# A store of 128 equal rows in place of a flip by matmuls: relative-position bias tables in a decoder trunk

## The chip, the cores and the metric

The kernel runs on one core of a Trainium2 chip. The metric is the device time of one execution in microseconds (us). The program is written out engine by engine: TensorE (PE in the profile, PEld for its weight loads), VectorE (DVE), ScalarE (ACT), GpSimd (POOL), and SyncE (SP), whose queue issues every DMA of this kernel. The engines meet only through semaphores.

## The reference

One pre-norm layer over 512 tokens of width 2048, in float32: three groups of heads on one input projection (6 gated DeltaNet heads, 4 dilated-window softmax heads, 6 sparse-attention heads), an output projection, and a gated MLP. The part that matters here is the bias of the ten softmax heads. It depends only on the distance between query and key:

```
def rel_bucket(dist):
    max_exact = REL_BUCKETS // 2
    n = jnp.maximum(dist, 0)
    nf = jnp.maximum(n, 1).astype(jnp.float32)
    large = max_exact + (jnp.log(nf / max_exact) / math.log(REL_MAX_DIST / max_exact)
                         * (REL_BUCKETS - max_exact)).astype(jnp.int32)
    large = jnp.minimum(large, REL_BUCKETS - 1)
    return jnp.where(n < max_exact, n, large)
...
            logits = (jnp.einsum('bhqd,bhqjd->bhqj', qb, kg)
                      + tab[:, rel_bucket(dil * j)][None, :, None, :])
...
        logits = jnp.einsum('bgrqd,bgkd->bgrqk', qb, kb) + w_bias
```

So head h needs, for query row p of a block of 128 and column c, a value f_h(p - c + constant): a table in which each row is the row above it, moved by one column.

## The kernel before

The work is a chain of blocks. At the end of a block all engines wait for each other, and the next block starts only then. The first block (the L322 block) normalizes x, transposes it on TensorE and splits it into a high and a low part (`h_hi`, `h_lo`), and makes the bias tables. The second (the L412 block) is the DeltaNet heads, the third (L935) the four dilated heads, the fourth (L1042) the sparse heads; output projection and MLP follow. Through all of them one stream of weights flows: SyncE loads units of 1 MB into two buffers `w_raw` (`load_unit`, L146), ScalarE rounds quarters of them to `w_hi` (L173), VectorE takes the rest into `w_lo` (L182), and TensorE multiplies them with three matmuls for each 128 rows of the contraction (`project`, L221). The independent projections are laid between the dependent steps of the heads (`filler`), so that TensorE nearly always has something to do.

The bias tables take this way in the first block:

1. TensorE makes for each of the ten heads one row of 1024 values (two matmuls, L391), and VectorE copies them to SBUF into `rev`, which is rows 0 to 9 of the tile `onehot` (L379, L380).
2. SyncE stores these 10 rows of 4 KB to the DRAM scratch `rev_d` (L351; `bias_scratch` in the profile), and waits until they have landed.
3. SyncE reads them back in 16 pieces of up to 512 columns. Row p of a piece begins one element after row p-1: the step between rows is 1 (L356). The pieces lie where `xs`, the input, was, and so each round of 8 waits until x was used. Between the two rounds it loads the first two weight units.
4. The rows come out in the wrong order (the first should be the last). So TensorE multiplies each piece with a matrix `K_REV` that flips the 128 rows (L406), and VectorE copies the result back (L385). These are the last thing that both do in the block.
5. SyncE stores the 16 pieces to a second scratch, `toep_d` (L362; `toeplitz_scratch`), and waits at the end of the block until all have landed.

Block three loads the tables of its four heads with one DMA (L989, `dil_tab`), block four those of its six heads with one (L1210, `nsa_tab`), as aligned rows. Everything SyncE issues stands in one queue, in the order of the program. What is in that queue in the first block is the order of the `@block.sync` function below. ScalarE and VectorE have split eight quarters, two weight units, by the end of the first block; TensorE uses up one of the two there (L398) and starts the second block with the other.

Of the kernel before, what the change touches and what calls it, by code (L numbers as in the profile page):

```python
# [22 lines left out]
F32 = mybir.dt.float32  # L23
# [5 lines left out]
P = 128  # L29
# [5 lines left out]
DN_H, DIL_H, NSA_H, NSA_G = 6, 4, 6, 2  # L35
# [15 lines left out]
QW = 512  # L51
RING = 8
AHEAD = 4
TW_DIL, TW_NSA = 512, 896
YLEN = 1024
# [2 lines left out]

LEVELS = (2, 4, 8, 16, 32, 64)

(K_ID, K_ONE, K_TRI, K_ML, K_MU, K_M1, K_M1T, K_REV) = range(8)
K_LV = 8
N_CST = K_LV + len(LEVELS)

N_SMALL = 2 * DN_H + 3 * NSA_H
# [40 lines left out]
def program(nc, t):  # L106
    with ExitStack() as ctx:
        def sem(name):
            return ctx.enter_context(nc.semaphore(name))
# [10 lines left out]
        cst = sb(ctx, "cst", [P, N_CST, P])  # L120
# [3 lines left out]
        PB, W = bank[:4], bank[4:]  # L124
        ident, ones = cst[:, K_ID, :], cst[:, K_ONE, :]
        ob = [sb(ctx, f"head_out{g}", [P, SEQ]) for g in range(NSA_G)]
        mix_d = nc.dram_tensor("mix_scratch", (KT, P, SEQ), F32).ap()
        rev_d = nc.dram_tensor("bias_scratch", (DIL_H + NSA_H, YLEN), F32)


        raw_in = [sem("raw_in_even"), sem("raw_in_odd")]
# [110 lines left out]
        const_in, table_in = sem("const_in"), sem("table_in")  # L242
        stored = sem("stored")
# [70 lines left out]

        toep_d = nc.dram_tensor("toeplitz_scratch", (DIL_H + NSA_H, P, TW_NSA), F32).ap()

        PIECES = [(h, 0, QW) for h in range(DIL_H + NSA_H)] + [(h, QW, TW_NSA - QW) for h in range(DIL_H, DIL_H + NSA_H)]
        ROUNDS = (PIECES[:8], PIECES[8:])  # L320

        with ExitStack() as c1, nc.Block() as block:  # L322
            xs = sb(c1, "xs1", [P, TB, D_MODEL])
            bl, oh = sb(c1, "bias_lhs", [BUCKETS + 2, DIL_H + NSA_H]), sb(c1, "onehot", [BUCKETS + 2, YLEN])
            rev = oh[0:DIL_H + NSA_H, :]
            id1 = sb(c1, "ident_first", [P, P])

            def piece(i, w):

                return xs[:, i // 4, i % 4 * QW:i % 4 * QW + w]  # L330

            x_in = [sem(f"x_in{b}") for b in range(TB)]
            const_ready, id_in, bias_in, rev_ps, rev_sb, piece_ps, piece_sb = (
                sem(n) for n in ("const_ready", "id_in", "bias_in", "rev_ps", "rev_sb", "piece_ps", "piece_sb"))
            g_row, g_in = sb(c1, "n1_g", [P, D_MODEL]), sem("n1_g_in")
            n1_act, n1_dve, n1_pe, n1_y, n1_lo = normalize(
                "n1", lambda e, b: e.wait_ge(x_in[b], 16), g_row, g_in, xs, c1, id1[:])

            @block.sync
            def _(sp):  # L340
                sp.dma_start(bl[:], t["bias_lhs"]).then_inc(bias_in, 16)
                sp.dma_start(oh[:], t["onehot"]).then_inc(bias_in, 16)
                sp.dma_start(xs[:, 0, :], t["x"][0:P, :]).then_inc(x_in[0], 16)
                sp.dma_start(id1[:], t["cst"][:, K_ID, :]).then_inc(id_in, 16)
                sp.dma_start(g_row[:], t["g1"]).then_inc(g_in, 16)
                sp.dma_start(xs[:, 1, :], t["x"][P:2 * P, :]).then_inc(x_in[1], 16)
                sp.dma_start(cst[:], t["cst"]).then_inc(const_in, 16)
                for b in range(2, TB):
                    sp.dma_start(xs[:, b, :], t["x"][b * P:(b + 1) * P, :]).then_inc(x_in[b], 16)
                sp.wait_ge(rev_sb, 1)  # L350
                sp.dma_start(rev_d.ap()[:, :], rev).then_inc(stored, 16)  # L351
                sp.wait_ge(stored, 16)
                for r, pieces in enumerate(ROUNDS):
                    sp.wait_ge(n1_y, 8 * (r + 1))
                    for i, (h, c, w) in enumerate(pieces):
                        sp.dma_start(piece(8 * r + i, w), bass.AP(tensor=rev_d, offset=h * YLEN + c, ap=[[1, P], [1, w]]))\  # L356
                            .then_inc(table_in, 16)
                    if r == 0:
                        load_units(sp, 2)
                for i, (h, c, w) in enumerate(PIECES):  # L360
                    sp.wait_ge(piece_sb, i + 1)
                    sp.dma_start(toep_d[h, :, c:c + w], piece(i, w)).then_inc(stored, 16)  # L362
                sp.wait_ge(stored, 16 + 16 * len(PIECES))

            @block.gpsimd
            def _(pool):
                nc.gpsimd.memset(eps_t[:], EPS).then_inc(const_ready, 1)
                nc.gpsimd.memset(one_t[:], 1.0).then_inc(const_ready, 1)

            @block.scalar  # L370
            def _(act):
                act.wait_ge(const_ready, 2)
                n1_act(act)
                split_hi(act, AHEAD + 4)

            @block.vector
            def _(dve):
                dve.wait_ge(rev_ps, 1)
                step(nc.vector.tensor_copy(rev[:, 0:512], W[0][0:DIL_H + NSA_H, :]))  # L379
                nc.vector.tensor_copy(rev[:, 512:1024], W[1][0:DIL_H + NSA_H, :]).then_inc(rev_sb, 1)  # L380
                n1_dve(dve)
                split_lo(dve, AHEAD + 4)
                for i, (h, c, w) in enumerate(PIECES):
                    dve.wait_ge(piece_ps, i + 1)
                    nc.vector.tensor_copy(piece(i, w), W[i % 4][:, 0:w]).then_inc(piece_sb, 1)  # L385

            @block.tensor
            def _(pe):
                pe.wait_ge(bias_in, 32)
                for i in range(2):  # L390
                    m = nc.tensor.matmul(W[i][0:DIL_H + NSA_H, :], bl[:], oh[:, i * 512:(i + 1) * 512],  # L391
                                         start=True, stop=True)
                m.then_inc(rev_ps, 1)
                pe.wait_ge(id_in, 16)
                n1_pe(pe)

                pe.wait_ge(n1_lo, 4 * TB)
                filler(pe, 1)(KT)  # L398
                pe.wait_ge(const_in, 16)
                pe.wait_ge(rev_sb, 1)  # L400
                for i, (h, c, w) in enumerate(PIECES):
                    if i % 8 == 0:
                        pe.wait_ge(table_in, 16 * (i + 8))
                    if i >= 4:
                        pe.wait_ge(piece_sb, i - 3)
                    nc.tensor.matmul(W[i % 4][:, 0:w], cst[:, K_REV, :], piece(i, w), start=True, stop=True)\  # L406
                        .then_inc(piece_ps, 1)

        STORED2 = 16 + 16 * len(PIECES)


        with ExitStack() as c2, nc.Block() as block:  # L412
# [522 lines left out]
        with ExitStack() as c3, nc.Block() as block:  # L935
            tab = sb(c3, "dil_tab", [P, DIL_H, TW_DIL])
# [31 lines left out]
            def dil_dve(dve, n, hd):  # L968
                settle(dve)
                dve.wait_ge(q_used, Q3 + 12 * n)  # L970
                nc.vector.tensor_scalar(qs[:], PB[0][:], SCALE, None, ALU.mult).then_inc(q_ev, 1)
                split_lo(dve, 2)
                dve.wait_ge(table_in, 16 * len(PIECES) + 16)

                def bias(a, e):
                    if isinstance(hd, int):
                        return tab[:, hd, a:e]
                    return tab[:, bass.ds(hd, 1), a:e].rearrange("p a n -> p (a n)")

                attend_dve(dve, n, lg, nm, den, bias, None, True, lambda k: split_lo(dve, 2 * k))  # L980
                split_lo(dve, 2)
                dve.wait_ge(att_o, n + 1)
                dve.wait_ge(stored, 16 * DN_H + STORED2 + 16 * n)
                nc.vector.tensor_copy(ob[0][:], PB[3][:]).then_inc(ob_v, 1)
                dve.wait_ge(ob_v, n + 1)

            @block.sync
            def _(sp):
                sp.dma_start(tab[:], toep_d[0:DIL_H, :, 0:TW_DIL].rearrange("h p c -> p h c")).then_inc(table_in, 16)  # L989
                for n in range(DIL_H):  # L990
                    load_units(sp, (Q3 + 12 * (n + 1) + AHEAD + 3) // 4)
                    sp.wait_ge(ob_v, n + 1)
                    sp.dma_start(mix_d[DN_H + n, :, :], ob[0][:]).then_inc(stored, 16)
# [48 lines left out]
        with ExitStack() as c4, nc.Block() as block:  # L1042
# [162 lines left out]
            def _(sp):  # L1205
# [1 line left out]
                sp.dma_start(w2[:], t["cmp_w2"]).then_inc(par4, 16)  # L1207
                load_units(sp, (Q_HEAD + AHEAD + 3) // 4)
                sp.wait_ge(q_used, Q_CMP + 2 * W1Q)
                sp.dma_start(tab[:], toep_d[DIL_H:, :, :].rearrange("h p c -> p h c")).then_inc(table_in, 16)  # L1210
                for r in range(NSA_R):
                    load_units(sp, (Q_HEAD + 8 * min(r + 1, NSA_R - 1) + AHEAD + 3) // 4)
                    if r == NSA_R - 1:
# [97 lines left out]
            def _(dve):  # L1311
# [50 lines left out]
                for g in range(NSA_G):  # L1362
                    dve.wait_ge(cm_k, 2 + g)
                    nc.vector.tensor_copy(vc[:, g, :], W[2 + g][0:N_CMP, 0:HD]).then_inc(cm_kv, 1)
                dve.wait_ge(table_in, 16 * len(PIECES) + 32)
                take_q(dve, 0)
                with repeat(dve, NSA_R - 1, (dve_q, 8, "nsa_dve quarters"), (dve_c, TICKS["nsa_dve"], "nsa_dve")) as r:
                    nsa_dve(dve, r, False)
# [294 lines left out]
def constant_tiles():  # L1663
# [9 lines left out]
    out[:, K_ML] = np.where(i > j, 0, BIG)  # L1673
    out[:, K_MU] = np.where(i <= j, 0, -BIG)
    out[:, K_M1] = level(1)
    out[:, K_REV] = i + j == P - 1
    out[:, K_M1T] = level(1).T
    for n, b in enumerate(LEVELS):
        out[:, K_LV + n] = level(b).T
# [107 lines left out]
```

## Time and profile before

| | us |
|---|---|
| median of 3 runs | 2793.23 (2792.86 to 2794.67) |
| the profiled execution, its own time | 2789.81 |
| its span in the trace | 2788.0 |
| granted TensorE clock, mean | 0.975 |
| TensorE busy | 2628.1 (94% of the span) |
| VectorE busy | 1315.3 (47%) |
| ScalarE busy | 874.3 (31%) |
| DMA: all queues | 259.34 MB, 93 GB/s on average |

The span begins with the first instruction that the trace shows. What lies between the span and the time of the execution is 1.8 us. The share of a DMA row is the mean over the core's 16 DMA engines.

### The profile page before, as it was taken

How to read it: one execution, taken by the hardware profiler on the slowest of the kernel's cores; microseconds unless marked ns; L12 is line 12 of the kernel's file. 1: busy time of each engine (PE TensorE's matmuls, PEld its weight loads, DVE VectorE, ACT ScalarE, POOL GpSimd, SP SyncE). 2: the span in 40 equal slices, each digit the busy share in tenths (PEclk: the TensorE clock that was granted, in tenths of full speed). 3: DMA queues.
4: the chain of work that ended last, by engine and by line, in shares of the span. 5: the costliest groups of instructions: out<-in, count | busy, mean ns of one | idle time of the engine just before them, and what ended most of it. 6: DMA issues, size and time to landing. Idle time of an engine off the chain costs nothing.

```text
span 2788.0 us, 33817 instructions
## 1 busy us (share of the span) xinstructions
PE 2628.1 (94%) x12024; PEld 2124.7 (76%) x12024; DVE 1315.3 (47%) x2196; ACT 874.3 (31%) x1628; POOL 77.0 (3%) x54
## 2 busy tenths in 40 slices
PE   6999989889999886998999999999999999999997
PEld 4777777777788553886888888888888888888886
DVE  5555666633244555334444444444344444444444
ACT  3433333323234333223332223232223232323223
POOL 0001111100000000000000000000000000000002
PEclk9999999999999996998999999999999999999999
DMA  6111111112235001521322222222222223222222
GB/s 239 72 65 34 60 64 64 49 65 98 76 117 208 14 38 68 204 99 57 110 101 98 97 91 91 106 94 103 91 91 91 102 95 106 91 92 103 91 94 91
DMA packets 44219, 259.34 MB, mean 93 GB/s; under 512 B 5136, under 2 KB 7056, under 8 KB 15292
## 3 DMA queue, kind: packets, MB, share of 16 engines
q1 hardware_dynamic: 44092, 257.62, 25.7%
q8 instruction: 83, 1.36, 0.2%
q14 instruction: 44, 0.36, 0.0%
HBM read 245.37 MB, written 12.23 MB: 92 GB/s over the span
## 4 chain that ended last, share of the span: by engine, by line
PE 52%; DVE 0%; ACT 0%; issue 0%; DVEq 0%; ACTq 0%
PE bank L221 34%; PE bank L1502 18%; ACT fin_squares L1606 0%; DVE xs L1649 0%; DVE xs L1648 0%; DVE xs L1564 0%; DVEq L1467 0%; ACT fin_rs L1609 0%; ACT L1609 0%; DVE fin_rs L1643 0%; ACTq L1605 0%; DVEq L1628 0%
## 5 line engine op out<-in xcount | busy, mean ns | idle before, releaser
L221 PE MATMUL bank<-h_hi,w_hi 128*128 128x512 f32 x2272 | 915.4, 403 | 12.2 <-DVE w_lo L182 6.9
L221 PE MATMUL bank<-h_lo,w_hi 128*128 128x512 f32 x2272 | 889.3, 391 | 0.0
L221 PE MATMUL bank<-h_hi,w_lo 128*128 128x512 f32 x2272 | 888.5, 391 | 0.0
L182 DVE TENSOR_TENSOR w_lo<-w_raw,w_hi 128x512 fp32r<-128x512 f32 x840 | 557.4, 711 | 470.5 <-ACT w_hi L173 468.9
L173 ACT ACTIVATE w_hi<-w_raw 128x512 fp32r<-128x512 f32 x840 | 489.5, 624 | 707.5 <-PE bank L1502 314.9
L221 PEld LDWEIGHTS bank<-h_hi,w_hi 128*128 128x128 f32 x2272 | 429.4, 189 | 103.0 <-issue 10.2
L221 PEld LDWEIGHTS bank<-h_lo,w_hi 128*128 128x128 f32 x2272 | 428.7, 189 | 91.8
L221 PEld LDWEIGHTS bank<-h_hi,w_lo 128*128 128x128 f32 x2272 | 429.5, 189 | 86.7 <-issue 3.2
L1502 PE MATMUL bank<-w_lo,g_hi 128*128 128x512 f32 x704 | 279.1, 396 | 0.0
L1502 PE MATMUL bank<-w_hi,g_lo 128*128 128x512 f32 x704 | 279.1, 396 | 0.0
L1502 PE MATMUL bank<-w_hi,g_hi 128*128 128x512 f32 x704 | 279.1, 396 | 0.0
L1564 DVE TENSOR_TENSOR xs<-xs,bank 128x512 f32<-128x512 f32 x176 | 120.9, 687 | 229.4 <-PE bank L1502 222.5
L1542 DVE SCALAR_TENSOR_TENSOR ffn_val<-bank,ffn_wg,ffn_val 128x511 f32<-128x511 f32 x44 | 33.0, 750 | 388.7 <-ACT ffn_val L1518 388.7
L1518 ACT ACTIVATE ffn_val<-bank,ffn_wg 128x512 f32<-128x512 f32 x44 | 30.3, 689 | 425.2 <-PE bank L221 425.2
L1502 PEld LDWEIGHTS bank<-w_lo,g_hi 128*128 128x128 f32 x704 | 132.6, 188 | 32.3
L1502 PEld LDWEIGHTS bank<-w_hi,g_lo 128*128 128x128 f32 x704 | 132.6, 188 | 32.3
L1502 PEld LDWEIGHTS bank<-w_hi,g_hi 128*128 128x128 f32 x704 | 132.6, 188 | 32.3
L1407 PE MATMUL bank<-w_hi,h_hi 128*128 128x512 f32 x256 | 101.0, 394 | 2.0 <-DVEq L1430 2.0
L1407 PE MATMUL bank<-w_hi,h_lo 128*128 128x512 f32 x256 | 100.6, 393 | 0.0
L1407 PE MATMUL bank<-w_lo,h_hi 128*128 128x512 f32 x256 | 100.5, 393 | 0.0
L1624 POOL TENSOR_TENSOR xs<-xs,gain_row 128x512 f32<-128x512 f32 x12 | 16.4, 1400 | 2200.9 <-ACT fin_squares L1606 2200.9
L790 POOL TENSOR_TENSOR dn_LT<-dn_AT,cst 128x512 f32<-128x512 f32 x36 | 60.3, 1709 | 488.2 <-ACT dn_AT L678 488.2
(274 smaller groups left out, 1992.3 us busy)
## 6 DMA issues: line engine op xcount, KB each, us to landing
w_raw<-in_weights SPq DMA_DIRECT2D x210, 1024.0 KB, 4.8
xs<-in_x SPq DMA_DIRECT2D x4, 1024.0 KB, 13.6
mix_scratch<-head_out SPq DMA_DIRECT2D x16, 256.0 KB
xs<-in_x SPq DMA_DIRECT2D x1, 4096.0 KB, 17.7
out<-xs SPq DMA_DIRECT2D x4, 1024.0 KB, 6.1
nsa_tab<-toeplitz_scratch SPq DMA_DIRECT2D x1, 2688.0 KB, 11.2
xs<-bias_scratch SPq DMA_DIRECT2D x10, 256.0 KB, 5.1
toeplitz_scratch<-xs SPq DMA_DIRECT2D x10, 256.0 KB
```

The costliest lines, as they stand in the source:

```text
L173: nc.scalar.activation(w_hi[:, act_q.n % RING, :], raw_quarter(act_q), ACT.Copy)\
L182: nc.vector.tensor_tensor(w_lo[:, s, :], raw_quarter(dve_q), w_hi[:, s, :].bitcast(F32), ALU.subtract).then_inc(lo_done, 1)
L221: m = nc.tensor.matmul(PB[pb][:], a[:, s, k], b[:, kt, :], start=(kt == 0 and n == 0), stop=(kt == KT - 1 and n == 2))
L790: nc.gpsimd.tensor_tensor(v3(LT[:, lv, :]), v3(B["AT"][:]), c3b(K_LV + lv), ALU.mult)\
L1407: m = nc.tensor.matmul(bank[4 * c + b][:], x[:, kt, b * P:(b + 1) * P], w[:, s, :], start=(kt == 0 and n == 0), stop=(kt == KT - 1 and n = ...
L1502: m = nc.tensor.matmul(W[b][:], x[:, slot, kt, b * P:(b + 1) * P], w[:, s, :], start=(kt == 0 and n == 0), stop=(kt == GT - 1 and n == 2))
L1518: nc.scalar.activation(dst[:], PB[2 * (j % 2) + v][:], ACT.Copy, scale=fwg[:, v, 2, j:j + 1])\
L1542: link(dve, nc.vector.scalar_tensor_tensor(dst[:, 1:SEQ], bk[:, 0:SEQ - 1], fwg[:, v, 1, j:j + 1], dst[:, 1:SEQ], ALU.mult, ALU.add))
L1564: nc.vector.tensor_tensor(dst, dst, W[b][:], ALU.add).then_inc(dn_free, 1)
L1624: nc.gpsimd.tensor_tensor(xs[:, b, cc], xs[:, b, cc], fg[:, cc], ALU.mult).then_inc(fin_g, 1)
```

## The change

The ten rows of 1024 are stored 128 times each: `rows_d` (`bias_rows` in a profile) holds 128 equal rows of 4 KB for each head, 5.24 MB in all, written by one DMA whose source repeats each SBUF row (step 0, count 128). From such a scratch a table in the right order can be read straight: it begins in the first row at column 127, and the step from row to row is 1023, one whole row less one element. So the pieces, the flip, its copies, the second scratch and the matrix `K_REV` are gone. Block three reads its tables with four DMAs instead of one, block four with six instead of one. The two weight units of the first block are now loaded ahead of the wait for `rev`. SyncE still waits in the first block until the store has landed.

```
-        rev_d = nc.dram_tensor("bias_scratch", (DIL_H + NSA_H, YLEN), F32)
+        rows_d = nc.dram_tensor("bias_rows", (DIL_H + NSA_H, P, YLEN), F32)
...
-        PIECES = [(h, 0, QW) for h in range(DIL_H + NSA_H)] + [(h, QW, TW_NSA - QW) for h in range(DIL_H, DIL_H + NSA_H)]
-        ROUNDS = (PIECES[:8], PIECES[8:])
+        STORED2 = 16
+
+        def load_table(sp, tab, heads, width):
+
+            for i, h in enumerate(heads):
+                src = bass.AP(tensor=rows_d, offset=h * P * YLEN + P - 1, ap=[[YLEN - 1, P], [1, width]])
+                sp.dma_start(tab[:, i, :], src).then_inc(table_in, 16)
...
+                load_units(sp, 2)
                 sp.wait_ge(rev_sb, 1)
-                sp.dma_start(rev_d.ap()[:, :], rev).then_inc(stored, 16)
-                sp.wait_ge(stored, 16)
-                for r, pieces in enumerate(ROUNDS):
-                    sp.wait_ge(n1_y, 8 * (r + 1))
-                    for i, (h, c, w) in enumerate(pieces):
-                        sp.dma_start(piece(8 * r + i, w), bass.AP(tensor=rev_d, offset=h * YLEN + c, ap=[[1, P], [1, w]]))\
-                            .then_inc(table_in, 16)
-                    if r == 0:
-                        load_units(sp, 2)
-                for i, (h, c, w) in enumerate(PIECES):
-                    sp.wait_ge(piece_sb, i + 1)
-                    sp.dma_start(toep_d[h, :, c:c + w], piece(i, w)).then_inc(stored, 16)
-                sp.wait_ge(stored, 16 + 16 * len(PIECES))
+                sp.dma_start(rows_d.ap()[:, :, :], rev[:, None, :].to_broadcast([DIL_H + NSA_H, P, YLEN]))\
+                    .then_inc(stored, 16)
+                sp.wait_ge(stored, STORED2)
...
-                for i, (h, c, w) in enumerate(PIECES):
-                    dve.wait_ge(piece_ps, i + 1)
-                    nc.vector.tensor_copy(piece(i, w), W[i % 4][:, 0:w]).then_inc(piece_sb, 1)
...
-                for i, (h, c, w) in enumerate(PIECES):
-                    if i % 8 == 0:
-                        pe.wait_ge(table_in, 16 * (i + 8))
-                    if i >= 4:
-                        pe.wait_ge(piece_sb, i - 3)
-                    nc.tensor.matmul(W[i % 4][:, 0:w], cst[:, K_REV, :], piece(i, w), start=True, stop=True)\
-                        .then_inc(piece_ps, 1)
...
-                sp.dma_start(tab[:], toep_d[0:DIL_H, :, 0:TW_DIL].rearrange("h p c -> p h c")).then_inc(table_in, 16)
+                load_table(sp, tab, range(DIL_H), TW_DIL)
...
-                sp.dma_start(tab[:], toep_d[DIL_H:, :, :].rearrange("h p c -> p h c")).then_inc(table_in, 16)
+                load_table(sp, tab, range(DIL_H, DIL_H + NSA_H), TW_NSA)
```

SyncE's queue in the first block of the kernel before, from the load of the constants (`cst`) to the first load of block two. `x2` is two alike in a row; a wait stands with the row that it holds.

```order
L347 DMA cst<-in_cst 128x1792
L349 DMA xs<-in_x 128x2048 x2
L351 DMA bias_scratch<-onehot 10x1024 [waits rev_sb]
L356 DMA xs<-bias_scratch 128x512 [waits n1_y,stored]
L356 DMA xs<-bias_scratch 128x512 x7
L146 DMA w_raw<-in_weights 128x2048 x2
L356 DMA xs<-bias_scratch 128x512 [waits n1_y]
L356 DMA xs<-bias_scratch 128x512
L356 DMA xs<-bias_scratch 128x384 x6
L362 DMA toeplitz_scratch<-xs 128x512 [waits piece_sb] x10
L362 DMA toeplitz_scratch<-xs 128x384 [waits piece_sb] x6
L322 UNCONDITIONAL_BRANCH [waits stored]
```

The same stretch of the changed kernel:

```order
L346 DMA cst<-in_cst 128x1664
L348 DMA xs<-in_x 128x2048 x2
L146 DMA w_raw<-in_weights 128x2048 x2
L351 DMA bias_rows<-onehot 1280x1x1024 [waits rev_sb]
L325 UNCONDITIONAL_BRANCH [waits stored]
L771 UNCONDITIONAL_BRANCH [waits barrier_Pool_Activation_PE_DVE_SP_release]
L773 DMA small_raw<-in_w_small 128x480
```

The two weight loads now stand right behind those of x; one store of 1280 rows of 1024 is all that remains of 33 DMAs, and the branch behind it still waits for `stored` and ends the block.

TensorE's queue at the end of the first block, as a difference: the last projection, the flip, and the branches to the next block.

```order
 L221 MATMUL bank<-h_hi,w_lo 128x512
 L221 MATMUL bank<-h_lo,w_hi 128x512
-L406 MATMUL bank<-xs,cst 128x512 x10
-L406 MATMUL bank<-xs,cst 128x384 x6
-L322 UNCONDITIONAL_BRANCH
-L809 UNCONDITIONAL_BRANCH
```

The 16 flips are gone, so the last work of TensorE in the first block is the last matmul of the projection.

## Rows read from the trace of the kernel before

**Rows 1.** The page: busy time, share, instructions; the chain by engine.

```profile
PE 2628.1 (94%) x12024; PEld 2124.7 (76%) x12024; DVE 1315.3 (47%) x2196; ACT 874.3 (31%) x1628; POOL 77.0 (3%) x54
...
PE 52%; DVE 0%; ACT 0%; issue 0%; DVEq 0%; ACTq 0%
```

**Rows 2.** Timeline of the first block: start, duration, engine, instruction, idle before.

```profile
11.51 0.67 DVE L380 COPY onehot<-bank 10x512 f32<-10x512 f32 x1
12.21 0.30 SPq L351 DMA_DIRECT2D bias_scratch<-onehot  x1
...
22.03 3.67 SPq L356 DMA_DIRECT2D xs<-bias_scratch  x8
25.74 1.01 SPq L146 DMA_DIRECT2D w_raw<-in_weights  x2
...
35.67 4.26 ACT L173 ACTIVATE w_hi<-w_raw 128x512 fp32r<-128x512 f32 x8
...
49.63 0.39 PE L221 MATMUL bank<-h_lo,w_hi 128*128 128x512 f32 x1
...
49.86 12.62 PE L406 MATMUL bank<-xs,cst 128*128 128x512 f32 x32
...
65.37 0.34 SPq L795 DMA_DIRECT2D small_raw<-in_w_small  x1
65.41 0.65 PE L221 MATMUL bank<-h_hi,w_hi 128*128 128x512 f32 x1 [2.94 <-PEq L322]
```

**Rows 3.** The DMA queue's own waits over the span: us, times, longest.

```profile
SPq L356 <- DMA bias_scratch<-onehot: 1.5, 1, 1.5
SPq L322 <- DMA toeplitz_scratch<-xs: 1.5, 1, 1.5
```

**Rows 4.** DMA packets in the stretch 18.5 to 19.25 us.

```profile
DMA packets 47, 0.16 MB, mean 208 GB/s; under 512 B 24, under 2 KB 24, under 8 KB 32
```

**Rows 5.** DMA packets in the stretch 21.2 to 21.5 us.

```profile
DMA packets 5, 0.01 MB, mean 27 GB/s; under 512 B 3, under 2 KB 3, under 8 KB 5
```

**Rows 6.** Stretches: busy us by engine, granted clock, DMA share, GB/s.

```profile
19.00:21.20 2.20, 0.41 (x3) 0.04 (x2) 2.20 (x5) 1.94 (x3) 0.00 (x0) 1.00 0.13 52
24.00:28.00 4.00, 2.34 (x16) 1.68 (x15) 4.00 (x8) 3.75 (x6) 0.00 (x0) 1.00 1.03 300
65.40:69.00 3.60, 3.59 (x9) 2.83 (x10) 0.37 (x1) 0.60 (x1) 0.00 (x0) 0.53 0.59 110
69.00:75.00 6.00, 6.00 (x28) 4.97 (x27) 0.29 (x1) 0.00 (x0) 0.00 (x0) 1.00 0.79 332
890.00:892.00 2.00, 2.00 (x11) 1.63 (x10) 0.93 (x3) 0.03 (x1) 0.00 (x0) 1.00 0.98 414
```

**Rows 7.** DMA issues: how many, KB each, median us to landing.

```profile
nsa_tab<-toeplitz_scratch SPq DMA_DIRECT2D x1, 2688.0 KB, 11.2
...
dil_tab<-toeplitz_scratch SPq DMA_DIRECT2D x1, 1024.0 KB, 5.5
...
onehot<-in_onehot SPq DMA_DIRECT2D x1, 136.0 KB
```

**Rows 8.** Timeline where the third block begins, to TensorE's first turn.

```profile
596.83 0.38 SPq L989 DMA_DIRECT2D dil_tab<-toeplitz_scratch  x1
...
604.92 1.15 ACT L173 ACTIVATE w_hi<-w_raw 128x512 fp32r<-128x512 f32 x2 [5.52 <-DMA w_raw<-in_weights]
...
606.79 0.28 DVE L890 TENSOR_TENSOR dil_lg<-bank,dil_tab 128x128 f32<-128x128 f32 x1
...
610.67 0.29 DVE L899 TENSOR_SCALAR dil_lg<-dil_lg,dil_den 128x128 f32<-128x128 f32 x1
...
611.15 0.27 PE L869 MATMUL bank<-cst,dil_lg 128*128 128x128 f32 x1
```

**Rows 9.** Tile nsa_tab: its load, and its first reader on VectorE.

```profile
L1172 DVE TENSOR_TENSOR cmp_lg<-bank,nsa_tab x24: 192/202/204, 915.8 to 1047.5; 128x31 f32<-128x31 f32 x24
...
L1210 SPq DMA_DIRECT2D nsa_tab<-toeplitz_scratch x1: 426/426/426, 891.1 to 891.1; - x1
```

More of the change, by code:

```diff
@@ L59 @@
 LEVELS = (2, 4, 8, 16, 32, 64)
-(K_ID, K_ONE, K_TRI, K_ML, K_MU, K_M1, K_M1T, K_REV) = range(8)
-K_LV = 8
+(K_ID, K_ONE, K_TRI, K_ML, K_MU, K_M1, K_M1T) = range(7)
+K_LV = 7
 N_CST = K_LV + len(LEVELS)
@@ L312, in normalize @@
             return act_part, dve_part, pe_part, y_v, lo
-        toep_d = nc.dram_tensor("toeplitz_scratch", (DIL_H + NSA_H, P, TW_NSA), F32).ap()
-        PIECES = [(h, 0, QW) for h in range(DIL_H + NSA_H)] + [(h, QW, TW_NSA - QW) for h in range(DIL_H, DIL_H + NSA_H)]
-        ROUNDS = (PIECES[:8], PIECES[8:])
+        STORED2 = 16
[3 more added lines that the diff above has]
+                sp.dma_start(tab[:, i, :], src).then_inc(table_in, 16)
         with ExitStack() as c1, nc.Block() as block:
@@ L326, in program @@
             id1 = sb(c1, "ident_first", [P, P])
-            def piece(i, w):
-                return xs[:, i // 4, i % 4 * QW:i % 4 * QW + w]
             x_in = [sem(f"x_in{b}") for b in range(TB)]
-            const_ready, id_in, bias_in, rev_ps, rev_sb, piece_ps, piece_sb = (
-                sem(n) for n in ("const_ready", "id_in", "bias_in", "rev_ps", "rev_sb", "piece_ps", "piece_sb"))
+            const_ready, id_in, bias_in, rev_ps, rev_sb = (
+                sem(n) for n in ("const_ready", "id_in", "bias_in", "rev_ps", "rev_sb"))
             g_row, g_in = sb(c1, "n1_g", [P, D_MODEL]), sem("n1_g_in")
@@ L400, in _ @@
                 pe.wait_ge(rev_sb, 1)
-                for i, (h, c, w) in enumerate(PIECES):
-                    if i % 8 == 0:
-                        pe.wait_ge(table_in, 16 * (i + 8))
-                    if i >= 4:
-                        pe.wait_ge(piece_sb, i - 3)
-                    nc.tensor.matmul(W[i % 4][:, 0:w], cst[:, K_REV, :], piece(i, w), start=True, stop=True)\
-                        .then_inc(piece_ps, 1)
-        STORED2 = 16 + 16 * len(PIECES)
         with ExitStack() as c2, nc.Block() as block:
@@ L972, in dil_dve @@
                 split_lo(dve, 2)
-                dve.wait_ge(table_in, 16 * len(PIECES) + 16)
+                dve.wait_ge(table_in, 16 * DIL_H)
                 def bias(a, e):
@@ L1364, in _ @@
                     nc.vector.tensor_copy(vc[:, g, :], W[2 + g][0:N_CMP, 0:HD]).then_inc(cm_kv, 1)
-                dve.wait_ge(table_in, 16 * len(PIECES) + 32)
+                dve.wait_ge(table_in, 16 * (DIL_H + NSA_H))
                 take_q(dve, 0)
@@ L1675, in constant_tiles @@
     out[:, K_M1] = level(1)
-    out[:, K_REV] = i + j == P - 1
     out[:, K_M1T] = level(1).T
```

## The prediction

> **What bounds the kernel now.** I read the page first. TensorE is busy 94% of the span and the chain of work that ended last lies on it alone [rows 1]. So a change counts only where TensorE stands still or does work that can go. The timeline of the first block shows both. The last projection ends at 49.63 + 0.39 = 50.0 us, then the flips run for 12.6 us, and the next projection starts at 65.41 after 2.94 us without work [rows 2]. Those 2.94 us come from SyncE: it issues the last store, waits 1.5 us for it [rows 3], then the blocks change. What stands between the last projection of block one and the first of block two is 65.4 - 50.0 = 15.4 us, and all of it belongs to the tables.
>
> **What is removed.** The flips, their copies, the pieces and the second store go. If nothing else held the block, it would end with the projection. What stays is the change of blocks itself. Of the 2.94 us, 1.5 are the landing, about 0.7 the last copy (as L380) and 0.3 the last issue (as L351) [rows 2, 3]; 0.5 us is left for it. TensorE would then restart at 50.5 instead of 65.4: 14.9 us less. It would also start warm. In the kernel before, the pause is followed by 3.6 us at a granted clock of 0.53, that is at the lower of its two levels, 1.2 GHz, for nearly all of it: 9 matmuls in 3.6 us, 0.40 each, where the next 28 take 6.0 us, 0.21 each, at 2.4 GHz [rows 6]. That is another 9 x 0.19 = 1.7 us. The gain without any wait for the store is 16.6 us.
>
> **What is added: one store.** SyncE still waits for it before it leaves the block, so its landing is the other thing that can end the block. Three things fix it.
>
> *When it starts.* It is issued at 12.2 us as before [rows 2], but all DMAs stand in one queue, and each DMA engine works its part in order. The kernel before shows this: the 40 KB of the old store were issued at 12.21, and SyncE saw them land at 22.03, 9.5 us later, the last 1.5 of them after nothing else was left to wait for [rows 2, 3]. Their ten packets of 4 KB leave when the loads of x have drained: eight in the stretch to 19.25 us (32 packets under 8 KB less 24 tiny ones) [rows 4] and two at 21.2 to 21.5 us (5 less 3) [rows 5]. In between, the DMA share is 0.13, two engines of 16, at 52 GB/s [rows 6]: two engines run late. Now two weight units, 2.1 MB, stand ahead of the store. One engine moves 414 / (0.98 x 16) = 26.4 GB/s [rows 6], and its part of 131 KB takes 5.0 us. The store starts at about 18.9 + 5.0 = 23.9 us on most engines, 26.3 on the two late ones.
>
> *On how many engines it runs.* The ten old packets went to the late pair and to eight others, one row to an engine: ten engines. The new store has the same ten source rows, so I count 128 packets of 4 KB, 524 KB, for each of ten engines. At 26.4 GB/s that is 19.9 us.
>
> *Whether ten neighbouring SBUF rows can feed ten engines.* No row shows this: the old store took one packet from each row and was over before a limit could show, and every transfer at full rate in this trace covers 128 SBUF rows. There, 16 engines and 128 rows are the same thing, eight rows to an engine, and 26.4 GB/s may be the limit of the engine or that of a path into SBUF which serves eight rows. If it is the engine's, the store takes 19.9 us. If it is the path's, what counts is how many of rows 0 to 9 share one: 2, 4 or 8 of them, for 39.8, 79.4 or 159 us. These are the bounds, 19.9 and 159. I take four, the middle one of the three splits that share. The Trainium skill, page "SBUF — State Buffer", section "Door 1: The DMA port swizzle", maps rows 0 to 3 to one port, 4 to 7 to another and 8 and 9 to a third, each of about 27 GB/s, and says that a narrow tile reaches only these ports; by it the sum is 79 us too, and by the count of engines alone it would be 20. No run shown here confirms that for a store.
>
> *Sum with four rows to a path.* 23.9 + 79.4 = 103.3 us; SyncE sees it 0.5 us later (21.5 to 22.03 above); 0.5 us for the barrier: block two starts at 104.3. TensorE stands still from 50.0 on, and restarts cold as it did before, so the clock gives nothing back. Against 65.4 this is +38.9 us. DVE, ACT and TensorE all have their next work behind the block's end, and nothing in block two can be brought forward, so no cover exists for it.
>
> **What moves: the weight loads.** They land before 24 us instead of after 30; ScalarE takes them at 35.67 in both cases, straight after its last piece of h [rows 2]. No gain. They don't delay x, which stands ahead of them.
>
> **What moves: the table reads.** Block three issues four DMAs in place of one, at about 0.46 us each (3.67 for eight [rows 2]), 1.4 us more for SyncE, but the DMA engines are still at the table then, so the weight unit behind it isn't held by the issue. The skewed reads of the old pieces ran at 300 GB/s, in the stretch 24 to 28 us [rows 6], where aligned loads make 414: 1 MB in 3.5 us, not 2.5. Behind the table waits the weight unit for ScalarE (604.92), then VectorE (606.79, and 610.67 + 0.29), then TensorE at 611.15 [rows 8], with 0.2 us to spare. So 0 to 0.8 us; if all of the issue came on top, 2. The old pieces of a head read one and the same 4 KB, the new ones distinct rows, so I take 0.4. In block four the table is issued at 891.1, lands 11.2 us later and is first read at 915.8 [rows 7, 9]: 13 us of room, against 5 x 0.46 = 2.3 of issue and about 2.5 of slower reading. Nothing.
>
> Sum: 38.9 + 0.4 = +39.3 us. The profiled execution would go from 2789.8 to 2829.1, and the median, which lies 3.4 above, from 2793.2 to about 2832.
>
> **The rivals.**
>
> *Ten engines at full rate.* The store lands at 23.9 + 19.9 = 43.8 us, on the late pair 46.2, plus 0.5: 46.7, before TensorE's 50.0. Then the gain is whole: -16.6 + 0.4 = -16.2, 2777 us. For it speaks that the old packets left on eight engines within the same 0.75 us [rows 4]; against it, that they may have been fetched earlier, while the loads ahead of them were still being written, so that one packet each proves little. This is the case on the other side. It decides as long as sharing costs less than (49.5 - 24.4) / 19.9 = 1.26 times the unshared time.
>
> *Two rows to a path.* 23.9 + 39.8 + 1.0 = 64.7 us, the same as 65.4 before: with the tables -0.3, 2793 us. The whole gain would be eaten, and TensorE would stand still where it flipped.
>
> *Eight rows to a path.* 23.9 + 159 + 1.0 = 184: +118.5 + 0.4, 2912 us.
>
> *The tables are late.* If the skewed reads were much slower than 300 GB/s, block three would pay. At half that rate 1 MB takes 7 us, 4.5 more: +4.3 us on top of any case. Distinct rows a whole row apart speak against it.
>
> **How the numbers follow.** Four rows 0.60; ten engines at full rate 0.27; two rows 0.08; eight rows or worse 0.05. A measurement of this kernel tells 0.2% (5.6 us) from no change. So slower 0.65, same 0.08, faster 0.27. The time is that of the likeliest, 2832. Its own range is 2824 to 2841 (the start of the store 3 us either way, the rate 25.5 to 27.2 GB/s, the tables 0 to 4). To hold 8 in 10 the range must take in the unshared case: 2774 to 2841.
>
> **What would show it.** In the profile after: a gap of TensorE behind its first projection, ended by the change of blocks, about 54 us long (no gap, or one under 1 us, for ten engines at full rate; 14 for two rows). SyncE waits for the DMA of `bias_rows` to about 104 us. The slices from 24 to 103 us show a low DMA rate: with ports shared some 66 GB/s (5.24 MB in 79 us), with ten engines 264 GB/s until 44 us and then nothing. Block two starts at 104 instead of 65.4, and everything behind it keeps its length, up to 1 us at 600. Wrong would be a store that spreads over another number of engines than ten, or one limited by neither engine nor path but by the DRAM side.

## The result, and the profile after

| | before | after |
|---|---|---|
| median | 2793.05 us (2792.00 to 2794.67, 4 runs) | 2838.85 us (2834.94 to 2839.31, 4 runs) |
| ratio, 95% interval | | 1.0160 (1.0143 to 1.0178) |
| profiled execution, its span | 2789.81, 2788.0 | 2834.94, 2833.2 |
| granted clock, mean | 0.975 | 0.967 |

The changed kernel is 1.6% slower: 45.8 us by the medians, 45.2 by the spans of the two traces.

The page of the changed kernel, busy time of the engines (against [rows 1]), and its largest group with the idle time in front of it and what ended that:

```profile
PE 2615.3 (92%) x11992; PEld 2114.8 (75%) x11992; DVE 1305.4 (46%) x2180; ACT 874.9 (31%) x1628; POOL 77.0 (3%) x54
...
L221 PE MATMUL bank<-h_hi,w_hi 128*128 128x512 f32 x2272 | 915.2, 403 | 65.3 <-PEq L325 55.8
```

TensorE works 13 us less than before and the kernel takes 45 us more: what came is a wait. Most of it is one wait of 55.8 us, ended by the change of blocks (line 325). The timeline shows where it lies (start, duration, engine, instruction, idle before it; against [rows 2]):

```profile
5.00 0.93 SPq L146 DMA_DIRECT2D w_raw<-in_weights  x2
11.89 0.94 SPq L351 DMA_DIRECT2D bias_rows<-onehot  x1
34.36 4.26 ACT L173 ACTIVATE w_hi<-w_raw 128x512 fp32r<-128x512 f32 x8
...
48.55 0.39 PE L221 MATMUL bank<-h_lo,w_hi 128*128 128x512 f32 x1
104.75 0.34 SPq L773 DMA_DIRECT2D small_raw<-in_w_small  x1
104.79 0.77 PE L221 MATMUL bank<-h_hi,w_hi 128*128 128x512 f32 x1 [55.85 <-PEq L325]
```

SyncE's own waits in the first 120 us say what it waited for at that line (us, times, longest; against [rows 3]):

```profile
SPq L325 <- DMA bias_rows<-onehot: 91.5, 1, 91.5
```

And three stretches: busy us by engine, then granted clock, DMA share and GB/s (the third against [rows 6]):

```profile
28.00:60.00 32.00, 16.73 (x72) 12.90 (x70) 12.26 (x20) 8.22 (x15) 0.00 (x0) 0.82 0.60 77
62.00:102.00 40.00, 0.00 (x0) 0.00 (x0) 0.00 (x0) 0.00 (x0) 0.00 (x0) 0.50 0.48 51
104.80:108.50 3.70, 3.70 (x9) 2.93 (x10) 0.00 (x0) 0.25 (x1) 0.00 (x0) 0.51 0.55 107
```

The last columns are the ones to read. A share of 0.60 is 9.6 engines of 16 busy, so ten engines do have the store, and yet they move 77 GB/s together, 7.7 each, where an engine alone moved 26.4 [rows 6]. After 62 us 7.7 engines are busy with 51 GB/s. Engines that count as busy at a low rate point to a limit that isn't theirs; experiments 1 to 3 test that. The third stretch is TensorE after the pause, at a granted clock of 0.51, the lower of its two levels.

The whole difference, block by block, from the two traces (each stretch from the first row of a block to that of the next):

| stretch | before | after | difference |
|---|---|---|---|
| to the start of block two | 65.37 | 104.75 | +39.4 |
| block two | 531.46 | 531.59 | +0.1 |
| block three | 163.65 | 164.69 | +1.0 |
| block four | 357.17 | 355.97 | -1.2 |
| block five | 199.49 | 199.67 | +0.2 |
| MLP, to its first output store | 1459.05 | 1464.72 | +5.7 |

These make 45.2. Block four took between 356 and 360 us in all kernels of this study, those with the old tables too, so the -1.2 means nothing. Block two took between 530 and 535 us in them, so the +0.1 is closer than it deserves. The 5.7 us in the MLP are a surprise: the change touches nothing there.

### The profile page after: what moved, and what is told of

Its sections match the earlier page's. It is cut to its first block, busy times and chain, and to the rows that moved or that the text cites. A ratio compares the mean times of both kernels' runs of the same rounds, so it can differ in the third digit from the quotient of the medians.

```text
span 2833.2 us, 33712 instructions
## 1 busy us (share of the span) xinstructions
PE 2615.3 (92%) x11992; PEld 2114.8 (75%) x11992; DVE 1305.4 (46%) x2180; ACT 874.9 (31%) x1628; POOL 77.0 (3%) x54
## 3 DMA queue, kind: packets, MB, share of 16 engines
q8 instruction: 87, 1.43, 0.2%
## 4 chain that ended last, share of the span: by engine, by line
PE 51%; issue 0%; DVE 0%; ACT 0%; DVEq 0%; ACTq 0%
PE bank L221 34%; PE bank L1480 17%; ACT fin_squares L1584 0%; DVE xs L1627 0%; DVE xs L1626 0%; DVE xs L1542 0%; DVEq L1445 0%; ACT fin_rs L1587 0%; ACT L1587 0%; DVE fin_rs L1621 0%; ACTq L1583 0%; DVEq L1606 0%
## 5 line engine op out<-in xcount | busy, mean ns | idle before, releaser
L221 PE MATMUL bank<-h_hi,w_hi 128*128 128x512 f32 x2272 | 915.2, 403 | 65.3 <-PEq L325 55.8
```

Source lines behind the costliest of these rows:

```text
L221: m = nc.tensor.matmul(PB[pb][:], a[:, s, k], b[:, kt, :], start=(kt == 0 and n == 0), stop=(kt == KT - 1 and n == 2))
```

## The experiments

The theory was that a path into SBUF serves four neighbouring rows and that the store, with its ten sources in rows 0 to 9, has three such paths. The rivals: the limit is the count of engines, or lies on the DRAM side (128 equal rows written from one source). For the 5.7 us the theory was the place of the code, and the rival that the long pause or the changed buffers cause it. Where a time is from one execution it is given as "one run".

### 1. Source rows 12 apart

The matmul that makes the ten rows gets a wider left side with zero columns between the heads, and so puts them into rows 0, 12, ... 108 of a tile of their own. The DMA is otherwise the same: ten rows, 128 times.

```
+STEP = 12
+ROWS = 9 * STEP + 1
...
-            rev = oh[0:DIL_H + NSA_H, :]
+            rev = sb(c1, "bias_out", [ROWS, YLEN])
...
-                sp.dma_start(rows_d.ap()[:, :, :], rev[:, None, :].to_broadcast([DIL_H + NSA_H, P, YLEN]))\
+                sp.dma_start(rows_d.ap()[:, :, :], rev[0:ROWS:STEP, None, :].to_broadcast([DIL_H + NSA_H, P, YLEN]))\
```

> The changed kernel with its ten source rows at SBUF partitions 0, 12, 24, ... 108 instead of 0 to 9. The bytes, the ten engines and the packets of the store stay the same. Theory (neighbouring SBUF rows share a path of 26 GB/s): ten rows far apart share nothing, the store moves 264 GB/s and lands at about 46 us, block two starts at about 49.5 instead of 104.8 us, and the time is 2839 - 55 = 2784 us. Rival (ten engines, the repeated source or the DRAM side limit the store): nothing changes, 2839 us, block two at 104.8.

Measured: 2782.97 us (2779.1 to 2784.2, 6 runs) against 2793.49 of the kernel before (12 runs), ratio 0.9961 (0.9948 to 0.9974). The stretch of the store, columns as above:

```profile
26.00:42.00 16.00, 11.50 (x44) 9.53 (x45) 14.71 (x25) 9.99 (x19) 0.00 (x0) 0.61 0.64 264
```

Its timeline at the change of blocks:

```profile
50.49 0.39 PE L223 MATMUL bank<-h_lo,w_hi 128*128 128x512 f32 x1
51.17 0.34 SPq L775 DMA_DIRECT2D small_raw<-in_w_small  x1
...
51.20 0.47 PE L223 MATMUL bank<-h_hi,w_hi 128*128 128x512 f32 x1 [0.32 <-PEq L327]
```

The same ten engines (0.64 x 16 = 10.2) move 264 GB/s instead of 77, the ten times 26.4 of the prediction's first rival. The store is over at 46.1 us, before the projection, and TensorE waits 0.3 us instead of 55.8. One DMA with the same bytes, the same count of packets and the same target takes some 23 us from its first packet to its last, in place of 80, when its source rows have moved. (They also lie in a tile of their own now; experiments 2 and 3 have the same kind of tile and are slow.) The count of engines is not the limit, nor is the DRAM side, nor that each row is read 128 times. The MLP kept its extra time here (1464.99 us), so that does not come from the pause.

### 2. Source rows 2 apart

Experiment 1 with `STEP = 2`: rows 0, 2, ... 18. Groups of four rows make five pairs of them.

> The same with the ten source rows at partitions 0, 2, 4, ... 18. Theory (four neighbouring rows share a path): two rows share each path, the store takes 39.8 us instead of 79.4 and ends at about 63 us, block two starts at about 64 us, and the time is 2839 - 40 = 2799 us; the rate is 132 GB/s from start to end, since all five paths have the same load. If rows shared in groups of eight, 79 us and 2839 us; if the store were limited by anything but the rows, 2839 us as well.

Measured: 2801.33 us, one run. Stretch of the store, and TensorE's wait for the change of blocks:

```profile
28.00:60.00 32.00, 18.18 (x73) 14.74 (x71) 13.02 (x22) 8.35 (x15) 0.00 (x0) 0.71 0.60 126
```

```profile
PE bank L223 <- PEq L327: 16.0, 1, 16.0
```

126 GB/s on ten engines is five times 25.2, five paths. Groups of eight rows would have made only three. The prediction's rival "two rows to a path" had 64.7 us for the start of block two; it was 66.4, since one of the pairs lies on the two engines that start late: from 64 to 65 us only two engines were still busy (share 0.12), with 25 GB/s together.

### 3. Source rows 8 apart

`STEP = 8`: rows 0, 8, ... 72. No two of them are neighbours, so groups of four alone would give ten paths and 264 GB/s. This run asks whether rows far apart can share too. The Trainium skill says so ("SBUF — State Buffer", section "Door 1: The DMA port swizzle"): a row and the one 32 above it have the same port, one 64 above has another.

> As the spread by 12, but with the ten source rows at partitions 0, 8, 16, ... 72. No two of them are within four of each other. Theory A (only neighbours within a group of four or eight rows share a path): nothing shares, the store takes 20 us as with step 12, 2783 us. Theory B (the port map of the Trainium skill, page SBUF - State Buffer, Door 1: a row and the one 32 further on share a port, a row and the one 64 further on don't): rows 0 and 32, 8 and 40, 16 and 48, 24 and 56 share, rows 64 and 72 have a port each; eight of the ten engines run at half rate, the store takes 40 us, 145 to 160 GB/s at first, and the time is 2801 us, as with step 2.

Measured: 2796.81 us, one run (the kernel before 2787.79, one run). Two stretches of its store:

```profile
26.00:42.00 16.00, 12.10 (x50) 9.78 (x51) 14.30 (x25) 9.11 (x17) 0.00 (x0) 0.68 0.62 161
56.00:60.00 4.00, 0.00 (x0) 0.00 (x0) 0.00 (x0) 0.00 (x0) 0.00 (x0) 0.50 0.49 102
```

161 is six times 26.8, and later 102 is four times 25.5. The map of the Trainium skill gives just that: rows 0 and 32, 8 and 40, 16 and 48, 24 and 56 share, 64 and 72 stand alone. That makes six paths, of which the two with one row are done first. So "rows that are not neighbours" is no rule for spreading; a step of 12 works because it meets ten different paths.

### 4. One store of 40 KB, then a copy from DRAM to DRAM

The ten rows are stored once, and a second DMA writes each of them 128 times from there. It has 128 as its outer count instead of ten, and no SBUF side.

```
-        STORED2 = 16
+        STORED2 = 32
...
-                sp.dma_start(rows_d.ap()[:, :, :], rev[:, None, :].to_broadcast([DIL_H + NSA_H, P, YLEN]))\
-                    .then_inc(stored, 16)
+                sp.dma_start(one_d.ap()[:, :], rev).then_inc(stored, 16)
+                sp.wait_ge(stored, 16)
+                sp.dma_start(bass.AP(tensor=rows_d, offset=0, ap=[[YLEN, P], [P * YLEN, DIL_H + NSA_H], [1, YLEN]]),
+                             bass.AP(tensor=one_d, offset=0, ap=[[0, P], [YLEN, DIL_H + NSA_H], [1, YLEN]])).then_inc(stored, 16)
```

> The changed kernel, but SyncE stores the ten rows once (40 KB), waits, and repeats them 128 times by one DMA from DRAM to DRAM with the 128 copies as its outer dimension. Theory (the limit is on the SBUF side of the store): the copy runs on all 16 engines at the full rate, 5.24 MB in 12.7 us, over at about 41 us, before TensorE ends at 48.9; 2784 us, like the spread rows. Rival (writing 5.24 MB to DRAM in rows of 4 KB is what is slow, about 77 GB/s): 68 us for the copy, block two at about 97 us, 2831 us.

Measured: 2784.70 us (2782.2 to 2786.2, 7 runs) against 2793.49 (12 runs), ratio 0.9971 (0.9959 to 0.9982). Stretch of the copy, and SyncE's waits for the two DMAs:

```profile
30.00:42.00 12.00, 8.20 (x29) 6.90 (x30) 10.92 (x18) 6.77 (x13) 0.00 (x0) 0.54 1.02 322
```

```profile
SPq L326 <- DMA bias_rows<-bias_one: 19.2, 1, 19.2
SPq L354 <- DMA bias_one<-onehot: 14.4, 1, 14.4
```

All 16 engines are busy and write the same 5.24 MB at 322 GB/s, in about 17 us where 12.7 were expected. The 14.4 us are the small store's wait behind the loads of x and the weights. After it the copy still ends before the projection. So the DRAM takes such a stream at more than four times the 77 GB/s of the changed kernel.

### 5. The kernel before, with the new store added

Nothing is taken away: the old tables stay, and the new store, which nobody reads, is issued ahead of the pieces' stores; the block waits for both.

> The kernel before the change, with the new store of 5.24 MB added behind the loads of the second round of pieces, waited for at the end of block one and read by nobody. The part that the change adds, alone. Theory (four rows share a path): its packets start at about 40 us, it runs 79.4 us to 120 us, the stores of the flipped pieces queue behind it for 9 us more on the busy engines, and block two starts at about 129 us instead of 65.4: 2857 us, with no gaps in the MLP, since no code is moved. Rival (the store would be fast where it doesn't meet other traffic, ten engines at full rate): over at 60 us, hidden, 2793 to 2797 us.

Measured: 2860.72 us, one run, against 2791.14 (15 runs). Stretch of its store, and TensorE's wait:

```profile
44.00:60.00 16.00, 16.00 (x54) 9.91 (x53) 6.22 (x9) 0.00 (x0) 0.00 (x0) 1.00 0.60 77
```

```profile
PE bank L222 <- PEq L324: 67.9, 1, 67.9
```

Again 77 GB/s on ten engines, at another time, with TensorE at full clock beside it. The low rate belongs to the store, not to what ran beside it in the changed kernel. Block two began at 131.7 us, 66 later than before: the stores of the pieces stand behind the long one on the same engines and had to wait for it too.

### 6. The changed kernel, with 16 matmuls in the pause

Now the 5.7 us. In the changed kernel the MLP stretch has four gaps of TensorE that the kernel before has not, at 1710.7, 1976.0, 2241.6 and 2507.1 us, all in one line. The last one in the timeline, and the wait as the profile names it ("issue": nothing that the profile shows):

```profile
2507.12 0.39 PE L221 MATMUL bank<-h_hi,w_hi 128*128 128x512 f32 x1
2508.73 0.50 PE L221 MATMUL bank<-h_hi,w_lo 128*128 128x512 f32 x1 [1.22 <-issue]
```

```profile
PE bank L221 <- issue: 4.1, 4, 1.2
```

Two such matmuls follow at 0.23 us; here it is 1.61. The four together are 4.8 us over the normal step. The same stretch before and after:

```profile
1317.10:2776.20 1459.10, 1454.19 (x6336) 1191.68 (x6336) 645.72 (x1035) 423.75 (x737) 16.37 (x12) 1.00 0.27 96
```

```profile
1356.70:2821.40 1464.70, 1455.66 (x6336) 1190.90 (x6335) 646.04 (x1035) 423.72 (x737) 16.37 (x12) 1.00 0.27 95
```

The stretch is 5.6 us longer at the same granted clock, and the other engines worked as long as before. TensorE stood idle for 4.1 us more and counts 1.5 us more as busy; where the 0.8 us lie that the four gaps don't hold wasn't located.

The gaps lie 265.3, 265.6 and 265.5 us apart, once per pass of TensorE's loop in the MLP, and TensorE's program has become shorter ahead of that loop (32 matmuls and their 32 weight loads fewer). So the loop stands at another place of the code. The experiment puts 16 matmuls, with a result that nobody reads, into the pause of the first block, where they cost nothing:

```
                 pe.wait_ge(rev_sb, 1)
+                for i in range(16):
+                    nc.tensor.matmul(W[i % 4][:], cst[:, K_ONE, :], xs[:, i // 4, i % 4 * QW:(i % 4 + 1) * QW],
+                                     start=True, stop=True)
```

> The changed kernel with 16 more matmuls of TensorE behind its first projection, whose results nobody reads; TensorE stands still there anyway. It puts back the length of TensorE's program. It is for the 5 to 6 us that the changed kernel loses in the MLP, where its trace has four gaps of 1.2 to 1.6 us, one in each new pass of the loop, with no releaser. Theory (where the program's code falls decides whether a pass waits for code): the gaps are gone and the time is 2839 - 5 = 2834 us. Rival (clock or chance): the gaps stay or come and go between runs, 2839 us. Block two starts at 104.8 in both.

Measured: 2833.23 us (2830.7 to 2837.0, 4 runs) against 2793.49, ratio 1.0150 (1.0133 to 1.0167); the changed kernel without them had 2838.85. Its MLP stretch:

```profile
1361.20:2820.50 1459.30, 1454.34 (x6336) 1191.48 (x6335) 645.89 (x1035) 424.58 (x737) 16.41 (x12) 1.00 0.27 96
```

More work, less time: the four gaps are gone (no "issue" wait in that line), block two still starts at 104.8, and the MLP is as long as before.

### 7. Experiment 1, with 16 small matmuls ahead

The same cure on the version with spread rows; the matmuls are of one element each, and stand where TensorE waits for its first inputs.

```
+                pe.wait_ge(const_ready, 2)
+                for _ in range(16):
+                    nc.tensor.matmul(W[2][0:1, 0:1], one_t[:], one_t[:], start=True, stop=True)
                 pe.wait_ge(bias_in, 32)
```

> Both findings so far in one kernel: the ten source rows at partitions 0, 12, ... 108 (first run: 2783 us), and 16 matmuls of one element on TensorE while it waits for its first input, whose result nobody reads, so that TensorE's program is as long as before the change. Theory of the code's place: the four gaps in the MLP go, 5 us less than the spread rows alone, 2778 us, and nothing is paid for the 16, since TensorE waits there for about 7 us. Rival (the padded kernel was faster by chance or by its busier TensorE): 2783 us, gaps still there.

Measured: 2775.71 us (2773.6 to 2778.1, 4 runs) against 2791.14 (15 runs), ratio 0.9941 (0.9926 to 0.9956). The MLP takes 1459.05 us, without gaps; against the kernel before, experiment 1 stood at 0.9961. With both repairs the change does what it could: -15.4 us, where the prediction's rival with ten engines at full rate had -16.2.

### 8. The kernel before, its code moved

If it is the place of the code and nothing of the change, the kernel before can be given the gaps. The change had shifted TensorE's code by 64 instructions of the trace (12024 + 12024 became 11992 + 11992). 48 one-element matmuls ahead of the first ones (32 before the wait for `bias_in`, 16 before that for `id_in`) shift it by 192 the other way. The two places are 256 instructions apart; that they are alike is an assumption, and the run tries it.

> The kernel before the change, with 48 matmuls of one element on TensorE in its waits of the first 15 us, read by nobody. They move all later code of TensorE by 192 instructions, which against the 16 KB pieces in which the trace shows code being loaded is the same place as that of the changed kernel (64 instructions less). Theory (the place of the MLP loop's code in these pieces makes the gaps): the kernel before gets the four gaps too, MLP 1464 instead of 1459 us, 2798 us (up to 3 us more if the 48 don't fit in the waits). Rival (something else in the changed kernel makes the gaps): MLP stays 1459 us, 2793 us.

Measured: 2795.41 us (2791.7 to 2800.4, 11 runs) against 2791.14 (15 runs), ratio 1.0015 (1.0006 to 1.0024). Its MLP stretch, and the wait:

```profile
1322.90:2786.80 1463.90, 1455.46 (x6336) 1191.45 (x6336) 646.02 (x1035) 423.85 (x737) 16.41 (x12) 1.00 0.27 96
```

```profile
PE bank L221 <- issue: 3.5, 4, 1.0
```

Four gaps of TensorE, at 1677.0, 1942.4, 2207.7 and 2472.9 us, in a kernel that computes its tables in the old way. The MLP takes 4.8 us more. Block two starts at 66.4, 1.0 later, behind the added matmuls, which adds up to 5.8; the medians show 4.3, in the midst of a scatter of some 9 us. (The traced execution took 2800.37 us; block two was 3.2 us longer in it than before, at the upper end of its 530 to 535.) One more count goes along with it: the page's row of the queue for instructions. Before, after, and this kernel:

```profile
q8 instruction: 83, 1.36, 0.2%
```

```profile
q8 instruction: 87, 1.43, 0.2%
```

```profile
q8 instruction: 88, 1.44, 0.2%
```

One piece is 16 KB (1.43 MB / 87), and the kernels with gaps (after, experiments 1 to 4, this one) have 87 or 88 of them, those without (before, 5, 6, 7, 9) 83: four or five more, with four gaps. The pieces' times say where the extra ones lie. In the changed kernel one moves from 1709.5 us, as it does at the same place of the MLP in the kernel before; then comes the gap, until 1711.89; and a further piece moves from 1713.3, 1.4 us after the gap has ended. The kernel before has no such piece there. While TensorE stood idle no DMA packet moved at all, in any of the eight gaps of these two traces:

```profile
DMA packets 0, 0.00 MB, mean 0 GB/s; under 512 B 0, under 2 KB 0, under 8 KB 0
```

So it is shown that the place of TensorE's code makes the gaps, and that one more piece is loaded behind each of them. That TensorE waits in the gap for code is likely, but no trace shows the wait itself.

### 9. One DMA for the tables, on top of experiment 7

The tables of a block are read by one DMA whose source has the head as a dimension of its own, in place of four and six.

```
-            for i, h in enumerate(heads):
-                src = bass.AP(tensor=rows_d, offset=h * P * YLEN + P - 1, ap=[[YLEN - 1, P], [1, width]])
-                sp.dma_start(tab[:, i, :], src).then_inc(table_in, 16)
+            src = bass.AP(tensor=rows_d, offset=heads[0] * P * YLEN + P - 1,
+                          ap=[[YLEN - 1, P], [P * YLEN, len(heads)], [1, width]])
+            sp.dma_start(tab[:], src).then_inc(table_in, 16)
```

> The same, and each block's tables are read by one DMA again instead of four or six, from the same skewed scratch. It separates the two parts of the 1 us that block three is longer since the change: four issues of 0.5 us or slower reading. If the issues were the cause, block three goes back from 164.7 to 163.7 us and the time to 2777 us; if it is the reading, block three stays at 164.7 and the time at 2778 us.

Measured: 2775.50 us (2774.9 to 2776.1, 5 runs) against 2791.14, ratio 0.9943 (0.9929 to 0.9957). Its row of DMA issues for the tables of block three (count, KB each, median us to landing; before it took 5.5 [rows 7]):

```profile
dil_tab<-bias_rows SPq DMA_DIRECT2D x1, 1024.0 KB, 5.8
```

Block three takes 163.94 us here, against 164.56 in experiment 7 and 163.65 before. The other traces say more than this one pair: in the seven kernels that read the table with four DMAs (the changed one, experiments 1 to 4, 6, 7) it took 164.6 to 165.4, in the three with the aligned table and one DMA (before, 5, 8) 163.65, 163.94 and 163.79. With one DMA the skewed table is as fast as these. So the three further issues cost about 1 us, and nothing is left that could be put down to the skewed rows. Nor do the landings tell them apart: aligned 5.5, 5.8 and 5.4 us in those three, skewed 5.8. In the whole time (2775.50 against 2775.71) the difference can't be told. This and experiment 7 are the fastest kernels of the study.

## Why the prediction was right

It said 2832 us, with 2824 to 2841 for its likeliest case; it was 2838.85. The step that carries it, four source rows on one path, held and is shown by experiments. That the time lies in the narrow range owes something to luck: 5.7 us of it came from the MLP, which is no term of that range, and with these gaps gone (experiment 6) it is 2833.23. Step by step:

- **The start of the store.** Predicted 23.9 us. Two packets of its size (9 less 7 tiny ones) leave in the half microsecond to 23.5, and 26 (35 less 9) in the next: half a microsecond early, else right. The packets of the two stretches:

```profile
DMA packets 33, 0.20 MB, mean 410 GB/s; under 512 B 7, under 2 KB 7, under 8 KB 9
```

```profile
DMA packets 37, 0.12 MB, mean 246 GB/s; under 512 B 9, under 2 KB 9, under 8 KB 35
```

- **Ten engines.** Shares of 0.60 to 0.64 in the five kernels above with ten source rows, whatever their spacing, as long as all ten rows had packets left, and 1.02 in the one with an outer count of 128. Right. (The Trainium skill, "DMA: Bandwidth & Descriptors", section "Why a DMA increments its semaphore by 16 and not by 1", has a transfer split over the largest number of engines, up to 16, that divides the outer dimension on both sides: ten here, 16 for 128 copies; the shares agree.)
- **Four rows to a path.** This was chosen among 1, 2, 4 and 8, with no row to decide it, and all of the time hangs on it; as far as the rows of the kernel before go, the choice was a lucky one. Predicted end 103.3 us, last packet at 103.7; block two at 104.3, measured 104.75. The shape had been given as a flat 66 GB/s. It is 77 until rows 8 and 9 are through, at 62 us, and 51 from then on: three paths of 25.7 and two of 25.5. The mean and the end are the same, since four rows of 524 KB on one path set them. Experiments 1 to 3 show the path (264, 126 and 161 GB/s for other rows with nothing else changed).
- **The first rival** was right in its own sum: with ten paths the store ended at 46.1 us (46.2), and the whole came out at -15.4 with the code in place.
- **The restart.** TensorE starts at 0.51 of its clock, as it did before at 0.53 [rows 6]: nothing given back, as said. Where the pause is gone TensorE does start warm. In experiment 1 the first 3.6 us of block two hold 16 matmuls at a granted clock of 1.00, against nine at 0.53 before [rows 6]: seven more at 0.21 us each are 1.5 us, where the rival had 1.7:

```profile
51.20:54.80 3.60, 3.60 (x16) 2.99 (x17) 0.00 (x0) 0.24 (x1) 0.00 (x0) 1.00 0.48 101
```

- **The weights.** ScalarE took them at 34.36, not at 35.67, and the first block's projection ended 1.1 us earlier, at 48.9. The other kernels with early weights have 34.7 to 36.0 there, so that is scatter and the prediction's "no gain" stands; the wait for the store would have swallowed it anyway.
- **The tables.** +0.4 predicted, +1.0 measured in block three, and for the other reason. The prediction charged the skewed reading and let the issue go free ("the weight unit behind it isn't held by the issue"); experiment 9 shows the issue of four DMAs to cost about 1 us and the reading nothing that can be told. Block four: nothing, as predicted.
- **The term that was missing.** That "everything behind it keeps its length" failed in the MLP: +5.7 us, the larger part of the 6.8 us between the prediction and the median. Removing 16 matmuls moved TensorE's code, and its loop then stood still once per pass. Experiments 6 and 7 take that away, 8 brings it about in the kernel before. That it waits there for a piece of code fits the counts but isn't seen. Why just this line stalls, and at which places of the loop it would not, wasn't settled; that places 256 instructions apart are alike was tried at one shift only.

## What to carry to other kernels

A DMA that repeats a few SBUF rows is priced by the fullest of the paths under its source rows as soon as rows share one, not by its bytes or its engines: look for a share that is high at a rate that is low, and spread the rows (here a zero-padded matmul, for nothing) or replicate from DRAM. Before a table of 5 MB is written to save 15 us of flips, ask what the queue must wait for at the end of the block. Nothing reads this store before block three, some 530 us after it has ended; a kernel that waits for it only there was not run, and the loads of block two would then stand behind the store on its ten engines. And when a stretch that an edit doesn't touch changes its length, compare its waits named "issue" and the packets of the instruction queue: a few instructions more or less ahead of a loop were worth 5 us here.

## What the runs showed of the hardware

- Ten source rows, 5.24 MB, ten DMA engines: 77 GB/s from rows 0 to 9, 126 from 0, 2, ... 18, 161 from 0, 8, ... 72, 264 from 0, 12, ... 108. A path carries 25 to 27 GB/s. The six paths of the third fit rows 32 apart that share one, and rows 64 apart that don't.
- 128 copies of each of ten rows from DRAM to DRAM: 322 GB/s on 16 engines.
- After a pause of 56 us TensorE's first 3.7 us ran at a granted clock of 0.51, nine matmuls; after one of 0.3 us 3.6 us held 16, at 1.00.
- Skewed reads, each row from its own row of 4 KB and offset by one element: 5.8 us to land for 1 MB, aligned 5.4 to 5.8. Four issues in place of one made the block about 1 us longer.
- TensorE's loop lost 1.0 to 1.4 us once per pass, 4.8 us in all, when its code stood at another place; with the four stalls came four or five more pieces of 16 KB in the instruction queue, none of them moving during a stall.
